# Two projections turned round: products of 128x512 by token and 8 transposes each, in a gather-fed two-layer encoder step

## The reference, cut to what matters

```python
p = rms_norm(x, g_mix) @ w_in                      # 1024 -> 2176 columns
u_pool, c_val, c_gate, s_h, s_b, s_c = split(p)    # 256, 384, 384, 384, 384, 384
z  = c_val * sigmoid(c_gate)                       # depthwise conv of width 31, layer norm, silu
ya = pooled windows of u_pool @ w_pool ; yc = s_b * conv3(s_c * s_h)
x += concat(ya, yb, yc) @ w_out
h  = rms_norm(x, g_ffn)
q  = (h @ w_q).reshape(T, 8 heads, 2, 64)
s  = q . sub_keys                                  # 128 scores per head and half
ids, gates = top 16 of the sums of the two top 16  # 128 experts per token
act = gelu(h . expert_u[ids]);  x += sum(gates * act * expert_v[ids])
```

## Time and profile before

| | us |
|---|---|
| median of 3 runs | 3544.69 |
| lowest, highest | 3543.48, 3548.05 |
| profiled execution, its own time | 3569.21 |
| its span, first to last instruction | 3567.2 |
| VectorE busy | 2174.3 (61%) |
| GpSimd busy, gathers | 2157.2 (60%) |
| TensorE busy, pipelined | 2266.5 (64%) |
| ScalarE busy | 240.9 (7%) |
| mean granted TensorE clock | 0.797 of 2.4 GHz |
| HBM over the span | 336 GB/s |

### The profile page before, as it was taken

The page is one execution under the profiler, slowest core; times in us unless marked ns, Lnnn a source line. Parts: engine busy times, 40 slices in busy tenths (PEclk is TensorE's granted clock), DMA queues, the critical chain, the costliest instruction groups (busy, mean ns, idle before and its releaser), DMA issues.

```text
span 3567.2 us, 28278 instructions
## 1 busy us (share of the span) xinstructions
PE 2266.5 (64%) x9574; PEld 1003.0 (28%) x9574; DVE 2174.3 (61%) x5644; ACT 240.9 (7%) x479; POOL 2157.2 (60%) x2184
## 2 busy tenths in 40 slices
PE   7124766466765675577868365847687763655487
PEld 6113314131412161223314122512431412100011
DVE  3987288766656775645467866772706777755600
ACT  3000100100000000000100000000010000000000
POOL 0365566656665655567567655565756675666665
PEclk9656888788887857689989686668899886977699
DMA  6587798989898989997898989798789988999998
GB/s 232 218 331 281 283 362 319 394 310 370 315 384 338 339 316 401 397 410 285 317 368 320 385 301 345 269 370 328 293 316 362 342 322 335 367 380 390 378 376 327
DMA packets 331610, 1201.64 MB, mean 337 GB/s; under 512 B 40898, under 2 KB 41290, under 8 KB 329418
## 3 DMA queue, kind: packets, MB, share of 16 engines
q0 software_dynamic: 313344, 1140.99, 84.7%
q1 hardware_dynamic: 17034, 49.94, 3.7%
q10 hardware_dynamic: 1088, 8.91, 0.6%
HBM read 1188.82 MB, written 10.87 MB: 336 GB/s over the span
## 4 chain that ended last, share of the span: by engine, by line
POOL 27%; PE 22%; issue 18%; DVE 17%; another core or an unknown queue 9%; DMA 6%; ACT 1%; ACTq 0%; POOLq 0%; DVEq 0%
POOL rows L579 27%; PE acc L936 6%; PE psB L883 4%; DMA rows<-in_expert_v,idsT 4%; PE psB L788 4%; PE psA L788 4%; DVE rows L1383 4%; DVE work L1198 1%; DVE work L1112 1%; DVE work L1191 1%; DVE work L1188 1%; PE psA L779 1%; DVE work L1195 1%; DVE work L1232 1%
## 5 line engine op out<-in xcount | busy, mean ns | idle before, releaser
L936 PE MATMUL acc<-rows,strip 128*32 128x512 f32 x4352 | 1396.2, 668 | 681.5 <-DMA rows<-in_expert_v,idsT 510.6
L579 POOL DMA_INDIRECT rows<-in_expert_v,idsT x1088 | 1121.8, 1031 | 694.8 <-issue 298.3
L1383 DVE CUSTOM_DVE_ANT_0 rows<-rows,psH 128x1024 f32<-128x1024 f32 x1088 | 1289.6, 1219 | 372.4 <-DMA rows<-in_expert_u,ids 279.7
L579 POOL DMA_INDIRECT rows<-in_expert_u,ids x1088 | 1034.3, 951 | 700.2 <-issue 315.0
L936 PEld LDWEIGHTS acc<-rows,strip 128*32 128x32 f32 x4352 | 266.9, 116 | 1661.1 <-DMA rows<-in_expert_v,idsT 840.7
L788 PE MATMUL psB<-hT,w_in_sb 128*128 128x128 f32 (+1 forms) x1152 | 185.4, 320 | 112.8 <-issue 111.7
L883 PE MATMUL psB<-hT,w_q_sb 128*128 128x128 f32 x1152 | 175.2, 309 | 123.6 <-issue 82.3
L788 PE MATMUL psA<-hT,w_in_sb 128*128 128x128 f32 (+1 forms) x1280 | 197.4, 315 | 53.6 <-issue 53.6
L788 PEld LDWEIGHTS psB<-hT,w_in_sb 128*128 128x128 f32 x1152 | 174.8, 236 | 152.6 <-issue 149.9
L1112 DVE SCALAR_TENSOR_TENSOR work<-zbuf,chan,work 128x128 f32<-128x128 f32 (+1 forms) x870 | 214.5, 324 | 2.5 <-DVE work L1135 1.2
L788 PEld LDWEIGHTS psA<-hT,w_in_sb 128*128 128x128 f32 x1280 | 187.3, 232 | 78.3 <-issue 78.2
(11 more groups left out here) (177 smaller groups left out, 1236.9 us busy)
## 6 DMA issues: line engine op xcount, KB each, us to landing
rows<-in_expert_u,ids POOLq DMA_INDIRECT x1088
rows<-in_expert_v,idsT POOLq DMA_INDIRECT x1088
w_in_sb<-in_w_in ACTq DMA_DIRECT2D x4, 2176.0 KB, 14.7
w_in_sb<-in_w_in SPq DMA_DIRECT2D x4, 2176.0 KB, 14.6
w_out_sb<-in_w_out SPq DMA_DIRECT2D x2, 4096.0 KB
w_q_sb<-in_w_q SPq DMA_DIRECT2D x2, 4096.0 KB, 24.7
x_out<-x_mid SPq DMA_DIRECT2D x10, 512.0 KB
x_mid<-x_mix SPq DMA_DIRECT2D x8, 512.0 KB
```

Of the source, the lines that this page charges most:

```text
L579: nc.gpsimd.indirect_dma_start(out=rows[:, j, :], out_offset=None, in_=table[:, :], in_offset=bass.IndirectOffsetOnAxis(ap=index, axis=0))\
L936: last = nc.tensor.matmul(acc[LS * a:LS * (a + 1), half:half + 512], strip[:, first:first + LS], rows[:, at % RING, half:half + 512], star ...
L1383: nc.vector.tensor_tensor_reduce(rows[:, j, :], rows[:, j, :], psH[:, :], 1.0, 0.0, ALU.mult, ALU.add, dots[:, r:r + 1]).then_inc(s_free[j ...
```

## The change

The two groups of 64 products are turned round for items 1 to 9: `hT` is now the stationary side, and 512 columns of `w_in` or `w_q` move past it. The result lies by token, so ScalarE copies it to SBUF, TensorE transposes its 8 blocks of 128x128, and the rest goes on as before. For u, values and gates the copy lies in `upper` and the transposes write to `psB`. For the queries the copy lies in `xb` (after the store of x is done), in two halves, the transposes write to `psA`, and the scores of the two halves change places (`psB` first). The next load of x waits for the query transposes and moves from tick 24 to tick 28. For the sample all four copies of the tokens are now projected; before, 32 columns of `hT` moved.

```diff
-STD2, NORM2, TURN_X1, HT2_SET, QUERY, SCORES, ROUTE, FINISH, LOAD_X = 20, 21, 22, 23, 24, 26, 27, 39, 24
+STD2, NORM2, TURN_X1, HT2_SET, QUERY, SCORES, ROUTE, FINISH, LOAD_X = 20, 21, 22, 23, 24, 26, 27, 39, 28
+    def turned(m, q):
+        return 2 * (m - 1) + q + 1
@@ sync: load_x(m), and the load of g_final alike
                     sp.wait_ge(s_xn2, m)
+                    if turned(m - 1, 1):
+                        sp.wait_ge(s_qtT, turned(m - 1, 1))
@@ scalar: mixer(m, tick)
+                if tick == PROJ_A + 1 and m:
+                    act.wait_ge(s_pAt, m)
+                    nc.scalar.copy(upper, psB[:, :]).then_inc(s_pAc, 1)
...
                     if outputs_state(m):
                         act.wait_ge(s_nso, 48 * state_count(m))
+                    act.wait_ge(s_xst, 16 * (m + 1))
                     for q in range(2):
-                        nc.scalar.copy(qT[:, 4 * q:4 * q + 4, :], tri(psB[:, 512 * q:512 * q + 512]))\
+                        cols = slice(512 * q, 512 * q + 512)
+                        nc.scalar.copy(xb[:, cols], psB[:, cols]).then_inc(s_qt, 1)
+                    for q in range(2):
+                        act.wait_ge(s_qtT, turned(m, q))
+                        nc.scalar.copy(qT[:, 4 * q:4 * q + 4, :], tri(psA[:, 512 * q:512 * q + 512]))\
                             .then_inc(s_qT, 1)
@@ tensor: mixer(m, tick)
+                if tick in (PROJ_A, PROJ_A + 1):
+                    for k in range(4 * (tick - PROJ_A), 4 * (tick - PROJ_A) + 4):
+                        pe.wait_ge(s_win[k // 2], 16 * (l + 1))
+                        for half in (0, 512):
+                            last = nc.tensor.matmul(psB[:, half:half + 512], hT[:, k, :], w_in[:, k, half:half + 512],
+                                                    start=k == 0, stop=k == DC8 - 1, skip_group_check=True)
+                        if k < DC8 - 1:
+                            yield
+                    if tick == PROJ_A + 1:
+                        last.then_inc(s_pAt, 1)
+                        yield
+                        pe.wait_ge(s_pAc, m)
+                        for c in range(DC8):
+                            last = turn(psB[:, c * P:(c + 1) * P], upper[:, c * P:(c + 1) * P])
+                        last.then_inc(s_pA, 1)
...
                     for k in range(4 * (tick - QUERY), 4 * (tick - QUERY) + 4):
-                        for h in range(HEADS):
-                            last = nc.tensor.matmul(psB[:, h * P:(h + 1) * P], w_q[:, k, h * P:(h + 1) * P], hT[:, k, :],
-                                                    start=k == 0 and h % 4 == 0, stop=k == DC8 - 1,
-                                                    skip_group_check=True)
+                        for half in (0, 512):
+                            last = nc.tensor.matmul(psB[:, half:half + 512], hT[:, k, :], w_q[:, k, half:half + 512],
+                                                    start=k == 0, stop=k == DC8 - 1, skip_group_check=True)
@@ tensor: SCORES
-                    for q, dst, made in ((0, psA, s_sc), (1, psB, s_sc2)):
+                    for q in range(2):
+                        yield
+                        pe.wait_ge(s_qt, turned(m, q))
+                        for h in range(4 * q, 4 * q + 4):
+                            last = turn(psA[:, h * P:(h + 1) * P], xb[:, h * P:(h + 1) * P])
+                        last.then_inc(s_qtT, 1)
+                    for q, dst, made in ((0, psB, s_sc), (1, psA, s_sc2)):
                         yield
                         pe.wait_ge(s_qT, copied(m, q))
@@ vector: top_keys(m, pair)
-                src = psB if q else psA
+                src = psA if q else psB
```

More of the change, by code:

```diff
@@ L323, in build @@
         s_u0 = sem("first_u_made")
+        s_pAt = sem("u_val_gate_by_token_made")
+        s_pAc = sem("u_val_gate_by_token_copied")
         s_p2 = sem("first_tap_products_made")
@@ L381, in build @@
         s_h = sem("h_turned_back")
+        s_qt = sem("queries_by_token_copied")
+        s_qtT = sem("queries_turned")
         s_qT = sem("queries_copied")
@@ L535, in edges @@
                     sp.wait_ge(s_xn2, ITEMS)
+                    sp.wait_ge(s_qtT, turned(ITEMS - 1, 1))
                     sp.dma_start(xb[:, :], A["g_final"].rearrange("(a d) -> a d", a=1).partition_broadcast(P))\
@@ L809, in mixer @@
                         pe.wait_ge(s_hist, samples(m))
-                for first, dst, o, made in ((PROJ_A, psB, 0, s_pA), (PROJ_B, psA, D, s_pB)):
-                    if tick in (first, first + 1):
-                        for k in range(4 * (tick - first), 4 * (tick - first) + 4):
-                            last = project(m, dst, o, k)
-                            if k < DC8 - 1:
-                                yield
-                        if tick == first + 1:
-                            last.then_inc(made, 1)
+                if tick in (PROJ_A, PROJ_A + 1):
[13 more added lines that the diff above has]
+                        last.then_inc(s_pA, 1)
+                if tick in (PROJ_B, PROJ_B + 1):
+                    for k in range(4 * (tick - PROJ_B), 4 * (tick - PROJ_B) + 4):
+                        last = project(m, psA, D, k)
+                        if k < DC8 - 1:
+                            yield
+                    if tick == PROJ_B + 1:
+                        last.then_inc(s_pB, 1)
                 if tick == PROJ_C:
@@ L902, in mixer @@
                                 if is_sample(m):
-                                    to, t, o = psA, slice(h // 2 * LS, (h // 2 + 1) * LS), 512 * half + NK * (h % 2)
+                                    to, t, o = psB, slice(h // 2 * LS, (h // 2 + 1) * LS), 512 * half + NK * (h % 2)
                                 last = nc.tensor.matmul(to[t, o:o + NK], qT[r, h, t], keys[r, h, :],
```

## The result

| | before | after |
|---|---|---|
| median of 6 runs each, us | 3546.4 | 3523.3 |
| lowest, highest, us | 3542.4, 3570.9 | 3516.2, 3538.7 |
| profiled execution, its own time, us | 3569.2 | 3516.2 |
| mean granted TensorE clock | 0.797 | 0.808 |

The ratio is 0.9922, 95% interval 0.9896 to 0.9948: 28 us (18 to 37) faster. I had said 3501 in 3455 to 3565. The two profiled executions differ by 53 us, because the one of before is at the slow end of its runs (3542 to 3571) and the one of after is the fastest of its six. A difference of two profiles is not the gain; I use them for places, and other kernels' traces for sizes.

The account below looks back on a forecast made before the run. Bound taken: the gathers' DMA queues, so only their idle time can be won. Terms -38 - 6 + 6 - 18 = -56 us on the profile, taken as 44 for runs: 3544.7 - 44 = 3501 us, range 3455 to 3565.

Parts of the forecast that it names:

- What bounds the kernel: Whole kernel: the gathers' DMA queue sets the floor, 84.7% share; only time in which gathers stand still can be won.
- Queries of items 2, 3, 6, 9, -38: Query products before the scores: fewer instructions end slow single steps, idle DMA time comes back; 38 us saved.
- Rival 3: Query group: slow pace goes by time, so the change doesn't cure it; 5 us won in each of four, 3550; chance 0.12.
- Items 4 and 7, -6: Queries of the sample items, V rows beside: the small remaining stalls at L883 shrink; 6 us saved for both.
- items 1, 5, 8, +6: Queries without U rows or slow passes: added transposes and copies lengthen the chain, 2 us each; 6 us lost.
- PROJ_A, -18: First projection (u, values, gates): idle DMA in samples and item 1's delay won back, less longer chains; 18 us saved.
- 16 for idle DMA of the samples: PROJ_A of sample items 4 and 7: idle DMA time won back if the granted clock rises; some 16 us saved.
- 10 for item 1: Item 1's PROJ_A group takes 79 us, a clean one 15, delaying second projection and first V row; 10 us saved.
- -8 for chains: PROJ_A: added copy, transposes and signals make VectorE wait, 24 us engine time; a third, 8 us, lost.
- From the profile to the runs: Whole kernel: half the profiled time's 24.5 us excess over the median taken as stalls, so runs gain 44 instead of 56.
- Rival 1: Whole kernel: TensorE's slow single steps come only from recording; runs see the new chains, 18 us slower, 3563; chance 0.23.
- Rival 2: Whole kernel: slow steps shrink but the full gather queue sets the time; 20 us saved less 14, 3539; chance 0.13.

Follow-up runs that it names:

- three: The change with PROJ_B also turned by token in all items but the first, against the kernel before on chip D: 3517.7 us, ratio 0.9845.
- q_only2: Only the queries turned, PROJ_A as before, against the kernel before on chip D: 3561.6 us, ratio 0.9948.
- a_only: Only PROJ_A turned, queries as before, load of x at tick 24, against the kernel before on chip B: 3208.6 us, ratio 0.9956.
- q_only: Only the queries turned, PROJ_A as before, load of x at tick 28, against the kernel before on chip B: 3229.5 us, ratio 1.0018.
- a_sample: PROJ_A turned in the two sample items only, against the kernel before on chip C: 3546.0 us, ratio 0.9988.
- a_padb: PROJ_A turned, queries as before, samples' PROJ_B moving all 128 columns, against the kernel before on chip C: 3521.8 us, ratio 0.9929.
- q256: The change with query passes of 256 columns, 64 passes instead of 32, against the kernel before on chip D: 3551.7 us, ratio 0.9928.
- halves_padb: The change with column halves one after the other and samples' PROJ_B moving 128 columns, against the kernel before on chip D: 3531.5 us, ratio 0.9866.
- pad_ab: The kernel before with samples' PROJ_A and PROJ_B moving 128 columns instead of 32, nothing turned, against before on chip C: 3529.9 us, ratio 0.9964.
- a0_after: The change itself, unaltered, against the kernel before on chip B: 3209.7 us, ratio 0.9956.

## Why the prediction was right in sign and 22 us too low

**What bounds the kernel: held.** The gathers' queue, and the time in which they stand still. The share went from 84.7% to 85.7%, and is 86.0% in three, the fastest.

**Queries of items 2, 3, 6, 9, -38: the step that failed.** I wrote that 80 instructions "fit into what stood ready", so that the queries would be ready at the pace of the records and each wait be 4.5 to 5 us. The records did what I said, 32 passes in 16.15 us with no single steps. The signal didn't follow them: it came 14 to 20 us behind the last pass. In these items the end of the group came with the end of the burst of gathers, with 32 passes as with 64, and what the small group saved is the passes that had been left when the burst was over. That was 63 in 8.99 us. The copy came 18.4 - 10.0 = 8.4 us earlier after the last U row, the longer chain took 2.8 back (5.7 from copy to MAX8, was 2.9; my sum for that chain had been 4.5), and 5.6 us each is left, 23 in all at the waits. Of them 12 reach the intervals of the items, as far as the scatter there lets one say. Rival 3 had just this for the queries, "5 us won in each of four". I gave it 0.12. It failed as a total, because it charged 26 us of chains and credited PROJ_A with nothing.

**Items 4 and 7, -6; items 1, 5, 8, +6.** The first can't be told from PROJ_A's effect in the same items (q_only2 has 14 us less there than before, on another chip). The second didn't come: from first query pass to MAX8 takes 27.45 us in all three after the change, and took 26.7 to 27.7 before. The steps on top are hidden, and I had charged 2 us each.

**PROJ_A, -18.** The pieces were 16 for idle DMA of the samples, 10 for item 1 and -8 for chains. Item 1: 9.8 in the profiles, 8 in the means above. The samples: a_only against q_only 20 us less on chip B; before to after 27 on A, with the queries' part in it. The chains: over the items that aren't samples VectorE's wait for PROJ_A went down on A, from 61.9 to 30.8 us, so they don't show there; on B, with no crawl to hide them, it is 33.9 in a_only where q_only has 23.7. By these traces the part is worth more than I took. By runs it is 14 us where nothing crawls, with LOAD_X left at 24. Where it does crawl, a_only didn't run, a_sample can't be told from no change, and a_padb, with the wide PROJ_B on top, gains 25; so how much of the 28 us is PROJ_A's on A isn't shown by runs. The mechanism was the right one in kind, clock and idle DMA, and I had it for PROJ_A itself only. That PROJ_B behind it stays at 0.55 I had not looked at, and by single traces it held another 4 to 17 us (samples in the table: 636 for the change, 632 in a_padb, 619 in three). That the forecast came within 22 us is in part luck: the queries' term was far too large, and PROJ_A's, by the traces, too small.

**From the profile to the runs.** I halved the excess of the profiled time over the median. Nothing supports that it belongs to the stalls: before's runs on chip A reach 3570.9, and on C they spread from 3526 to 3575. The profiled run was one at the slow end of such a spread. Without the halving I would have said 3544.7 - 56 = 3489, 34 us too low.

**Rival 1, the crawl made by the recording: not for these chips.** The same recording shows no crawl on B and much on A, C and D, and the times go with it. Where nothing crawls its total is wrong too: it said 18 us slower, and on B the change is 14 faster. Only its charge at the scores has something to it, the 6 us of q_only. Every run here lists a span and a clock, so an execution without any recording is not among them, and what it would do stays open. **Rival 2** was at 3539: not reached, but part of it may be true, since of the 23 us at the waits about 12 reach the items. **V rows that meet the same crawl** I had named as a way to be wrong; it was PROJ_B instead, 105.0 us of "issue" where before had 53.6 in that group.

**What I said would show it:** no single steps, held. Waits of about 5 us, failed. PROJ_A's clock above 0.8 in samples, held (0.83, 0.80). Wait for the first projection under 60 us, held (49.4). Scores of items 1, 5, 8 later by 2 us, failed.

**Left open:** what delays TensorE's work and signals under the burst. It is not the recording alone, not the count between 32 and 64 at the queries, and not the share of the DMA engines alone: on chip B the gathers run at 409 GB/s and 1.03 with no crawl. It is not simply the end of the burst either, as item 1's PROJ_A, item 3 of q256 and the first half in halves_padb show. Gathers of half the size, or a burst that goes on past the queries, were not run.

## What to carry to other kernels

A group whose stalls look like slow issue may be held by something that ends elsewhere; ask what ends at the same moment, and credit a smaller group only with what is left to run after that moment. The end of a matmul in the records is modelled, so read when its consumer starts. And look at the granted clock of a group with few moving columns: making it wide, even with columns nobody reads, was worth 13 us (4 to 21) on chip C without any other edit, and it may also matter for the group behind. And a gap on "issue" isn't always slow issue: look up in the kernel what the instruction waits for, as PROJ_C waited for z in three.

## What the hardware showed that I had not expected

- One program, four chips: 3224, 3546, 3549 and 3575 us for the kernel before. The faster chip moves the same bytes at 373 GB/s instead of 338 and shows neither the crawl nor late signals. An edit that trades a longer chain for fewer instructions has the other sign there: q_only 1.0018 on B (1.0007 to 1.0030), 0.9948 on D (0.9906 to 0.9990).
- A signal 14 to 28 us behind the recorded end of the work that gives it, under full gathers (items 1, 2, 3, 6 and 9 of after), while the first 16 passes of item 6 in halves_padb signal 2.7 us behind theirs.
- A pass of 128 columns at a clock of 0.93 takes less than one of 32 at 0.55: 17.88 us busy for 129 (pad_ab) against 24.86 for 128 (after).
- The clock gained by one group lasted into the next in a_only on chip B (PROJ_B 0.72 and 0.76), little in a0_after on the same chip (0.59 and 0.58), and not in a_sample on C (0.54 and 0.50).
